# Seven quadrant products per double: sums kept in the banks on copies that ScalarE writes, and the products in another order

## The reference

```
h = h + 0.5 * ((silu(gate) * up) @ w_out)
gate, up = split(rmsnorm(h) @ w_in)        # 1024 -> 2 x 2816, then 2816 -> 1024
```

## Time and profile before

| | |
|---|---|
| median of 3 runs | 2158.23 us |
| the profiled execution's own time | 2158.83 us |
| its span, first to last instruction | 2157.0 us |
| PE / PEld / DVE / ACT busy | 99% / 88% / 72% / 41% |
| granted clock of PE, mean | 0.998 |

### The profile page before, as it was taken

One profiled execution on the slowest core, in us unless ns is written; L12 is line 12 of the kernel. 1 busy time (PEld: TensorE's weight loads), 2 busy tenths in 40 slices (PEclk: granted clock), 3 DMA queues, 4 the chain that ended last, 5 costly groups with the idle time before them and its releaser, 6 DMA issues.

```text
span 2157.0 us, 30584 instructions
## 1 busy us (share of the span) xinstructions
PE 2139.2 (99%) x12712; PEld 1900.5 (88%) x12712; DVE 1561.3 (72%) x1797; ACT 891.7 (41%) x1110; POOL 166.0 (8%) x135
## 2 busy tenths in 40 slices
PE   8999999999999999999999999999999999999998
PEld 6998998888777888998998898998788888998997
DVE  7975976453466548984898897697788768874983
ACT  6532443242233425541445543344572256442443
POOL 0000002610123100000000000000102002000002
PEclk9999999999999999999999999999999999999999
DMA  4332332232222223332242233223222123232241
GB/s 161 108 127 69 108 118 98 94 115 96 87 79 79 78 88 118 108 127 78 98 129 87 80 107 127 78 99 108 88 69 69 50 84 112 99 127 78 98 131 45
DMA packets 59176, 210.39 MB, mean 98 GB/s; under 512 B 6560, under 2 KB 8992, under 8 KB 58784
## 3 DMA queue, kind: packets, MB, share of 16 engines
q1 hardware_dynamic: 58464, 205.30, 28.3%
q0 software_dynamic: 288, 2.62, 0.3%
q10 hardware_dynamic: 288, 0.52, 0.1%
HBM read 206.33 MB, written 2.10 MB: 97 GB/s over the span
## 4 chain that ended last, share of the span: by engine, by line
PE 95%; DVE 2%; issue 1%; ACT 1%; DMA 0%; POOL 0%; POOLq 0%; SPq 0%; ACTq 0%; DVEq 0%
PE accs L669 26%; PE accs L671 26%; PE accs L670 26%; PE mixbs L671 3%; PE mixbs L670 3%; PE mixbs L669 3%; PE mixbs L1211 1%; PE mixbs L1234 1%; PE accs L1172 1%; PE accs L1171 1%; PE accs L1173 1%; DVE w_lo L1828 1%; PE mixbs L1056 0%; DVE h L1911 0%; DVE f_tmp L1906 0%
## 5 line engine op out<-in xcount | busy, mean ns | idle before, releaser
L1295 ACT ACTIVATE w_hi<-w_raw 128x1024 fp32r<-128x1024 f32 x497 | 515.4, 1054 | 600.5 <-PE accs L671 282.6
L1828 DVE TENSOR_TENSOR w_lo<-w_raw,w_hi 128x1024 fp32r<-128x1024 f32 x497 | 613.6, 1238 | 109.3 <-ACT w_hi L1295 102.9
L669 PE MATMUL accs<-x_hi,w_hi 128*128 128x512 f32 (+1 forms) x1408 | 491.9, 349 | 7.5 <-DVE x_lo L1895 7.5
L671 PE MATMUL accs<-x_hi,w_lo 128*128 128x512 f32 (+1 forms) x1408 | 485.2, 345 | 0.0
L670 PE MATMUL accs<-x_lo,w_hi 128*128 128x512 f32 (+1 forms) x1408 | 485.2, 345 | 0.0
L669 PEld LDWEIGHTS accs<-x_hi,w_hi 128*128 128x128 f32 x1408 | 267.8, 190 | 39.5 <-DVE x_lo L1895 8.2
L671 PEld LDWEIGHTS accs<-x_hi,w_lo 128*128 128x128 f32 x1408 | 267.7, 190 | 32.3
L670 PEld LDWEIGHTS accs<-x_lo,w_hi 128*128 128x128 f32 x1408 | 268.0, 190 | 30.4
L669 PE MATMUL accs<-hid_hi,w_hi 128*128 128x512 f32 (+1 forms) x714 | 275.8, 386 | 0.0
L670 PE MATMUL accs<-hid_lo,w_hi 128*128 128x512 f32 (+1 forms) x714 | 275.7, 386 | 0.0
L671 PE MATMUL accs<-hid_hi,w_lo 128*128 128x512 f32 (+1 forms) x714 | 275.6, 386 | 0.0
(11 more groups left out here) (405 smaller groups left out, 3080.1 us busy)
## 6 DMA issues: line engine op xcount, KB each, us to landing
w_raw<-weights SPq DMA_DIRECT2D x383, 512.0 KB, 3.2
y_t<-h SPq DMA_DIRECT2D x16, 128.0 KB, 1.9
h<-x_t SPq DMA_DIRECT2D x3, 512.0 KB, 7.2
k1c<-const POOLq DMA_DIRECT2D x1, 1536.0 KB, 7.7
k2c<-const POOLq DMA_DIRECT2D x1, 1024.0 KB, 8.2
h<-x_t ACTq DMA_DIRECT2D x2, 256.0 KB, 4.1
w_raw<-weights SPq DMA_DIRECT2D x1, 384.0 KB, 4.9
cst<-const SPq DMA_DIRECT2D x1, 161.0 KB, 8.9
```

What stands on the lines that cost most here:

```text
L669: pe.matmul(bank, w_hi[:, n % HI_SLOTS, w], hi, start=start, stop=False, skip_group_check=read_between)
L671: return pe.matmul(bank, w_lo[LO[n]][:, w], hi, start=False, stop=stop, skip_group_check=read_between)
L1295: act.activation(w_hi[:, n % HI_SLOTS, :], w_raw[RAW[n]][:, :], ACT.Copy).then_inc(hi_split, 1)
L1828: dve.tensor_tensor(w_lo[LO[n]][:, :], w_raw[RAW[n]][:, :], w_hi[:, n % HI_SLOTS, :].bitcast(F32), ALU.subtract).then_inc(lo_split, 1)
```

## The change

The products of a double are done in the order p1, p5, p6, p2, p7, then p1 of the next double, then p3 and p4. After the last double of a half the first output block stands in the place of the next p1. ACT writes minus p1 from r_a into r_b (neg); p6 adds to it there; ACT copies the sum to f_s (snap); p7 adds to r_b again, and later p4; p3 adds to p5 in r_c; ACT copies p5 to f_up before that (five), and the finished r_b to f_up at the end (c21). DVE has four operations on quadrants left: c11, c22 (`up_late`), c12 and gate (`gate_late`). The weight sums come in the order s3, s1, s2, s4, and the buffers of the weights go round in another way. P5 waits for all four mixed tiles at once, where p6 awaited them one by one. The core of the diff (removed lines stand in the functions above):

```diff
+PRODUCTS = ("p1", "p5", "p6", "p2", "p7", "p3", "p4")
+P1, P5, P6, P2, P7, P3, P4 = range(7)
...
+            UNITS[_d] = [_n + (_j + 1 if _j > P7 else _j - (2 if _i and _j == P1 else 0)) for _j in range(7)]
...
+def out_unit(f, p, u):
+    return FIRST[f"ffn{f}_out{p}"] + (u if u else -2)
...
+        def acted(d, name):
+            before = sum(2 if plain else 5 for e, n0, plain in ALL[:d])
+            return before + (["neg", "snap", "five", "silu", "c21"].index(name) if d in SEVEN else name) + 1
...
+            def quadrant(d, i, bank):
+                n = UNITS[d][i]
+                take_block(n)
+                for u in range(2):
+                    for k in range(KD // 2):
+                        hi, lo = operands(i, k)
+                        last = product(n, 4 * u + k, bank[:, u, :], hi, lo, i in (P1, P5) and k == 0, k == KD // 2 - 1,
+                                       read_between=True)
+                last.then_inc(block_done, 1)
+            def first_product(d, drain):
+                pe.wait_ge(*((drained, drain - 2) if drain else (quad, made(d - 1, "c11"))))
+                quadrant(d, P1, r_a)
+            def last_products(d):
+                pe.wait_ge(quad, made(d, "c22"))
+                quadrant(d, P3, r_c)
+                quadrant(d, P4, r_b)
+            def middle_products(f, d):
+                if SEVEN[d]:
+                    pe.wait_ge(quad, made(seven_before(d), "c12"))
+                if d % sum(HALVES) == NPLAIN[f]:
+                    pe.wait_ge(xm_done, 4 * f + KD // 2)
+                quadrant(d, P5, r_c)
+                pe.wait_ge(f_acted, acted(d, "neg"))
+                quadrant(d, P6, r_b)
+                quadrant(d, P2, r_a)
+                pe.wait_ge(f_acted, acted(d, "snap"))
+                quadrant(d, P7, r_b)
...
+                            first_product(d, drain)
+                            if i and d - 1 in SEVEN:
+                                last_products(d - 1)
+                            middle_products(f, d)
...
+                    out_tiles(f, p, range(1))
+                    last_products(d)
+                    out_tiles(f, p, range(1, 2 * HALVES[p]))
...
+            def quadrants_end(d):
+                act.wait_ge(quad, made(d, "gate"))
+                act.activation(f_gate[:, :, :], f_gate[:, :, :], ACT.Silu).then_inc(f_acted, 1)
+                act.wait_ge(block_done, UNITS[d][P4] + 1)
+                act.activation(f_up[:, :, t1], r_b, ACT.Copy).then_inc(f_acted, 1)
...
+                        split(at[P1] + 3)
+                        if not begins:
+                            split(at[P1] + 4)
+                            split(at[P1] + 5)
+                            quadrants_end(d - 1)
+                        act.wait_ge(block_done, at[P1] + 1)
...
+                        act.activation(r_b, r_a, ACT.Copy, scale=-1.0).then_inc(f_acted, 1)
+                        split(at[P5] + 3)
+                        split(at[P6] + 3)
                         if i:
                             round_hidden(d - 1)
+                        act.wait_ge(block_done, at[P6] + 1)
...
+                        act.activation(f_s[:, :, :], r_b, ACT.Copy).then_inc(f_acted, 1)
+                        split(at[P2] + 3)
...
+                        act.activation(f_up[:, :, t2], r_c, ACT.Copy).then_inc(f_acted, 1)
+                        split(at[P7] + 3)
+                    split(out_unit(f, p, 0) + 3)
+                    split(out_unit(f, p, 0) + 4)
+                    quadrants_end(d)
                     first = FIRST[f"ffn{f}_out{p}"]
                     for u in range(2 * HALVES[p]):
+                        if u == 1:
+                            round_hidden(d)
                         if u:
                             split(first + u + LEAD)
-                        else:
-                            round_hidden(d)
...
+                if n in DOUBLE_AT and DOUBLE_AT[n][1] == P1:
+                    weight_sum(DOUBLE_AT[n][0], "s3")
+                if n + 1 in DOUBLE_AT and DOUBLE_AT[n + 1][1] == P5:
+                    weight_sum(DOUBLE_AT[n + 1][0], "s1")
+                if n in DOUBLE_AT and DOUBLE_AT[n][1] == P5:
+                    weight_sum(DOUBLE_AT[n][0], "s2")
+                if n in DOUBLE_AT and DOUBLE_AT[n][1] == P2:
+                    weight_sum(DOUBLE_AT[n][0], "s4")
...
+                        if not begins:
+                            up_late(d - 1)
+                        prepare(at[P1] + 2)
+                        if not begins:
+                            prepare(at[P1] + 3)
+                            gate_late(d - 1)
+                            prepare(at[P1] + 4)
+                        prepare(at[P5] + 2)
+                        if not begins:
                             hidden(d - 1)
+                        prepare(at[P6] + 2)
+                        prepare(at[P2] + 2)
...
+                        prepare(at[P7] + 2)
                         if i:
                             hidden_rest(d - 1)
+                    up_late(d)
+                    prepare(start + 2)
+                    prepare(start + 3)
+                    gate_late(d)
+                    prepare(start + 4)
                     first = FIRST[f"ffn{f}_out{p}"]
                     for u in range(2 * HALVES[p]):
-                        prepare(first + u + LEAD)
-                        if u == 0:
+                        if u == 1:
                             hidden(d)
+                        if u:
+                            prepare(first + u + LEAD)
                         if u == 1:
                             hidden_rest(d)
```

More of the change, by code:

```diff
@@ L97 @@
 SEVEN = {d: i for i, d in enumerate(d for d, n0, plain in ALL if not plain)}
-DOUBLE_AT = {UNIT0[d] + i: (d, i) for d in SEVEN for i in range(7)}
+UNITS = {}
+for _f in range(4):
+    for _p in range(2):
+        _seven = [x for x in doubles(_f, _p) if not x[2]]
+        for _i, (_d, _n, _plain) in enumerate(_seven):
+            UNITS[_d] = [_n + (_j + 1 if _j > P7 else _j - (2 if _i and _j == P1 else 0)) for _j in range(7)]
+DOUBLE_AT = {n: (d, i) for d in UNITS for i, n in enumerate(UNITS[d])}
+def out_unit(f, p, u):
+    return FIRST[f"ffn{f}_out{p}"] + (u if u else -2)
 HID_COUNT = {d: sum(1 if plain else 2 for e, n0, plain in ALL[:d + 1]) for d in UNIT0}
@@ L144 @@
             _free[_slot] = FIRST["mo_conv"] + 3 if _name == "ffn3_in0" else FIRST["mix_out" if _slot == 4 else "ret_up"]
-    _n = FIRST[_name]
-    while _n < FIRST[_name] + _count:
+    for _n in range(FIRST[_name], FIRST[_name] + _count):
+        if _name.startswith("ffn") and "_out" in _name and _n == FIRST[_name]:
+            continue
         if _n in DOUBLE_AT:
-            _d = DOUBLE_AT[_n][0]
+            _d, _first = DOUBLE_AT[_n]
+            if _first != P1:
+                continue
             _a11, _a21 = _take((_d, "a11"), True), _take((_d, "a21"), True)
@@ L740, in operands @@
                 return xm_hi[:, k, x, :], xm_lo[:, k, x, :]
[L742 to L776, removed]
@@ L801, in plain_first, with out_tiles @@
                 dense(n + 3, a + 3, x_hi, x_lo)
-            def out_tiles(f, p):
-                first, out0, ds = FIRST[f"ffn{f}_out{p}"], OUT0[f"ffn{f}_out{p}"], [x[0] for x in doubles(f, p)]
+            def out_tiles(f, p, units):
+                out0, ds = OUT0[f"ffn{f}_out{p}"], [x[0] for x in doubles(f, p)]
                 for g, (m, k) in enumerate(OUT_SEQ[p]):
+                    if g // 8 not in units:
+                        continue
                     if f == 3 and p == 1 and m == KD - 1:
                         if k == 0:
-                            last_tile(g, first, out0 + m)
+                            last_tile(g, FIRST[f"ffn{f}_out{p}"], out0 + m)
                         continue
-                    n = first + g // 8
+                    n = out_unit(f, p, g // 8)
                     if g % 8 == 0:
@@ L1452, in ffn @@
                             continue
[L1453 to L1459, removed]
+                        at, begins = UNITS[d], d - 1 not in SEVEN or i == 0
@@ new lines, in ffn @@
+                        if begins:
+                            split(at[P1] + 2)
+                        split(at[P1] + 3)
[4 more added lines that the diff above has]
+                        act.wait_ge(block_done, at[P1] + 1)
+                        if begins:
+                            act.wait_ge(drained, OUT0[f"ffn{f}_in{p}"] + 4 * i)
+                        else:
+                            act.wait_ge(f_acted, acted(d - 1, "c21"))
@@ L1801, in weight_sum @@
                     out, one, two = P7, P1, P5
-                if name == "s2":
+                if name == "s1":
                     slot, count = LOADED[d, "a22"]
                     dve.wait_ge(loaded[slot], 16 * count)
+                    dve.wait_ge(w_summed, 4 * SEVEN[d] + 1)
+                    out, one, two = P5, P5, P4
+                if name == "s2":
```

(11 more changed lines are left out.)

90 lines of the change are left out of this document (32 added, 58 removed).

## The result

The changed kernel took 2166.03 us, the median of five runs (2165.59 to 2167.43), against 2158.16 us for the kernel before in the same session (2157.69 to 2158.63). The ratio is 1.0038, with a 95% interval of 1.0026 to 1.0049: slower by 0.4%. The profiled execution took 2165.59 us, its span 2163.7 us, 6.7 us more than before.

The account below looks back on a forecast made before the run. TensorE's stream was taken as the bound, with at most 1.4 us of waits to win. Ends 4.8 plus starts 1.1 and 0.7 made 6.6 us: 2165.4 profiled, 2164.8 median, range 2159.5 to 2168.5.

Parts of the forecast that it names:

- DVE removed: Seven quadrant operations per double become four: 79 us less DVE work beside PE, worth 0 to 1.4 us, taken as 0.
- ACT added: One copy of a bank per double becomes four: 68 us more on ACT, costing nothing while the negative copy stays under 2.0 us.
- steady order: Inner doubles: operands and loads are ready before PE needs them in the new product order; 0 gain, 0 loss.
- Cost of a copy into a bank: ACT's negative copy ahead of P6: taken as 0.60 us, from the nearest copy, bank to SBUF.
- Rival C: Copies into a bank are slow: from about 2.0 us P6 waits in 30 doubles; at 2.2 us, 6 us, 2171; chance 0.05.
- Ends: Ends of the four second halves: PE waits for hidden tiles ahead of output block 2, 1.2 us each, 4.8 in all.
- Rival A: The chain at the second halves' ends is shorter, under 0.6 us per end: total 4.6 or 3.7 us, 2162; chance 0.18.
- FFN 0's start: First half of FFN 0: a third weight sum delays the mixed tiles, so the first P5 starts 1.1 us late.
- FFN 2's start: First half of FFN 2: the second weight sum delays the reciprocal and the high part behind it, +0.7 us.
- FFN 1 and FFN 3: Starts of their first halves: the low part still ends before P5 is due despite the moved sum; 0 us.
- Rival B: DVE's relief speeds TensorE's stream to about 0.119 us per matmul: 8 us less, 2157, not slower; chance 0.05.

## Why the prediction was right, point by point

Faster 0.05, same 0.18, slower 0.77 stood on record, with 2164.8 us; measured 2166.03, in the range, 1.2 us above the point.

- *DVE removed, ACT added, steady order: 0.* Right, and shown: the inner doubles are at pace, and DVE's load put back changes nothing. Busy times came out at 1492 (forecast 1482) and 959 (960). The DVE term was 10 us off because I took 0.69 us for an operation, its full duration, where 114 fewer of them cut the busy time by 68.9 us, 0.60 each, overlaps taken out; this touches no wait.
- *Cost of a copy into a bank: 0.60.* Its group after:
```profile
L1478 ACT ACTIVATE f_up<-accs 128x512 f32<-128x512 f32 x38 | 22.8, 599 | 13.9 <-PE accs L693 13.9
...
L1501 ACT ACTIVATE accs<-accs 128x512 f32<-128x512 f32 x38 | 22.1, 582 | 12.0 <-PE accs L693 9.1
```
  582 ns into a bank against 599 into SBUF, both read from a bank. The Trainium skill ("ScalarE: Activation LUTs", Step-by-step: what each stage is for) calls PSUM the lower-latency destination; this trace agrees, by 17 ns, but only where the copy isn't queued right behind another: with two copies ahead of it, the copy into a bank took 591 ns (median), and the queued copy from mixbs to SBUF 589. Rival C is out by a wide margin, and the kernel with four copies shows that its place and mechanism were right: whatever stands ahead of P6 beyond the margin of 1.35 us is paid 30 times.
- *Ends, 1.2 us each.* Right in place, mechanism and size: 1.25 to 1.27, by what the stages lost when the waits were taken out. The chain of the end of FFN 0's second half, by DVE, ACT and PE, beside the earlier trace rows:
```profile
309.28 1.23 DVE L2026 TENSOR_TENSOR hid_f<-f_up,f_gate 128x1024 f32<-128x1024 f32 x1 [0.95 <-ACT f_up L1478]
312.58 1.23 DVE L1877 TENSOR_TENSOR w_lo<-w_raw,w_hi 128x1024 fp32r<-128x1024 f32 x1 [2.07 <-ACT w_hi L1323]
313.73 1.22 DVE L2031 TENSOR_TENSOR hid_lo<-hid_f,hid_hi 128x1024 fp32r<-128x1024 f32 x1
```
```profile
310.54 1.06 ACT L1540 ACTIVATE hid_hi<-hid_f 128x1024 fp32r<-128x1024 f32 x1 [1.29 <-DVE hid_f L2026]
311.51 1.99 ACT L1323 ACTIVATE w_hi<-w_raw 128x1024 fp32r<-128x1024 f32 x2
```
```profile
313.69 0.39 PE L693 MATMUL accs<-hid_hi,w_lo 128*128 128x512 f32 x1
315.09 0.47 PE L691 MATMUL accs<-hid_hi,w_hi 128*128 128x512 f32 x1 [1.01 <-DVE hid_lo L2031]
```
  From 309.28 to 314.95 is 5.67 us; before it was 5.66. The weight block's low part stands between, and DVE idles 2.07 us for that block's high part, ACT having taken two of them after the hidden round. Rival A, a shorter chain, is out, and taking the block out of the way removed the wait.
- *FFN 0's start, 1.1.* Right: 1.18, PE idle 0.94 with xm_lo as the releaser, forecast 0.9.
- *FFN 2's start, 0.7 more.* Right: 0.78. PE idles 1.95 us (forecast 1.8) for the low part of P5's weights. It is another wait than the one of 1.17 before, although the profile names the low part for both: before, that part was done at 1212.32, and P6, which writes accs, went 0.10 us after the multiply that read its bank ended (1212.91). P5 writes mixbs and does not wait for that multiply.
- *FFN 1 and FFN 3, 0.* Right: both stretches at pace.
- *Rival B, DVE's relief speeds the stream.* Out: 0.120 us per matmul with DVE at either load.
- *What was missing.* The sum gave 2165.4 us for a profiled execution, and that of the changed kernel took 2165.59. That it agrees to 0.2 us is in part luck: the three terms came out at 7.0 us for the 6.6 forecast, and the early start of FFN 0's stretch took 0.4 back. The point for the median was 1.2 us low because I took off the 0.6 us by which the profile of before stood above its median, while the profile after, the fastest of its five runs, stands 0.4 below its own: by their clocks two of the five carry a dip of TensorE's clock that the forecast did not have.

## What to carry to other kernels

When a product is moved in front of a wait, count what its neighbours on the *other* engines' queues do in the time it left: here one weight block, harmless two output blocks ahead of its use, cost 1.25 us four times, and moving one line behind another gave it back. Relief on an engine that nobody waited for was worth 0 here, 69 us of it, so judge a change of that kind by the new places in the queues that it makes. At the seams of a pipeline (first and last double) look up each hand-over by itself; the steady state tells nothing of them.

## What the runs showed that was not expected

The wait ahead of FFN 2's first P5 has a price behind it in some executions. In the profiled one of the kernel with the hidden tiles first, PE idles there for 1.95 us, runs at full pace for 1 us, then at half for 3.4 us (windows; the granted clock is the third number from the end):
```profile
1214.31:1215.35 1.04, 1.04 (x8) 1.04 (x9) 1.04 (x2) 0.98 (x2) 0.00 (x0) 0.98 0.70 284
1215.35:1218.77 3.42, 3.42 (x19) 3.42 (x18) 3.42 (x4) 1.05 (x2) 0.00 (x0) 0.51 0.01 4
1218.77:1230.00 11.23, 11.23 (x95) 11.23 (x95) 8.10 (x9) 5.60 (x7) 0.00 (x0) 1.00 0.26 88
```
That is the 1.2 GHz level (half of 2.4): 0.213 us per matmul in place of 0.120, 16 of them, 1.5 us. The same dip follows the same wait in the kernel with block 0 behind (0.54 over 3.42 us), and is not there in the profiled execution of the changed kernel, whose wait is 1.95 us too, nor in those with DVE's load or ACT's copies added. The timed runs fit: of the changed kernel's five, the two whose mean clock is 0.997 took 2166.94 and 2167.43 us, the three at 0.998 took 2165.59 to 2166.03. In the three kernels where that wait is 0.62 us or gone, no run of 33 is at 0.997, nor is one of the 42 of the kernel before that ran beside these experiments, whose wait is 1.17. That the dip makes those slower runs is inferred from their mean clock; only two profiles show it, and the mean clock is too coarse to sort single runs: the profiled execution with block 0 behind has the dip and reads 0.998. Why some executions have it and others with the same wait don't stays open.
